# Splitting the 64-column small matmuls of a triangular inversion into halves of 32 loaded columns

## The reference, cut to what matters

```python
l_mat = jnp.where(strict, jnp.einsum('bhncd,bhnjd->bhncj', kb, k) * decay, 0.0)
rhs = jnp.concatenate([v * beta[..., None], kb * jnp.exp(gc)[..., None]], axis=-1)
sol = lax.linalg.triangular_solve(jnp.eye(CHUNK, dtype=F32) + l_mat, rhs,
                                  left_side=True, lower=True, unit_diagonal=True)
```

## Time and profile before

| | |
|---|---|
| median of 3 runs | 2343.88 us (2343.21 to 2346.3) |
| profiled execution, its own time | 2346.62 us |
| its span in the trace | 2345.0 us |
| PE busy | 2319.4 us (99%), 14038 matmul records |
| PEld busy | 1883.7 us (80%) |
| DVE busy | 1270.6 us (54%) |
| ACT busy | 843.1 us (36%) |
| POOL busy | 113.3 us (5%) |
| granted TensorE clock | 0.996 |

### The profile page before, as it was taken

The page is one execution under the profiler, slowest core; times in us unless marked ns, Lnnn a source line. Parts: engine busy times, 40 slices in busy tenths (PEclk is TensorE's granted clock), DMA queues, the critical chain, the costliest instruction groups (busy, mean ns, idle before and its releaser), DMA issues.

```text
span 2345.0 us, 36491 instructions
## 1 busy us (share of the span) xinstructions
PE 2319.4 (99%) x14038; PEld 1883.7 (80%) x14038; DVE 1270.6 (54%) x1777; ACT 843.1 (36%) x1243; POOL 113.3 (5%) x220
## 2 busy tenths in 40 slices
PE   8999999999999999999999999999999999999998
PEld 6888888778777888888878888887777788888886
DVE  4554556675457664433465545667545576443333
ACT  4321234532455443223342223345225555331232
POOL 1000010020000000000000000001000000000000
PEclk9999999999999999999999999999999999999999
DMA  8564563342234344433345645624232352453331
GB/s 321 189 214 152 179 200 120 104 136 96 95 113 149 112 135 152 144 100 101 96 143 183 211 144 188 214 85 125 93 100 90 117 176 93 148 170 99 95 106 58
DMA packets 95152, 325.30 MB, mean 139 GB/s; under 512 B 12904, under 2 KB 13576, under 8 KB 94016
## 3 DMA queue, kind: packets, MB, share of 16 engines
q1 hardware_dynamic: 57456, 216.09, 28.1%
q0 software_dynamic: 23760, 82.48, 11.1%
q10 hardware_dynamic: 13824, 25.17, 3.1%
HBM read 306.34 MB, written 14.73 MB: 137 GB/s over the span
## 4 chain that ended last, share of the span: by engine, by line
PE 95%; DVE 2%; ACT 1%; DMA 1%; issue 0%; SPq 0%; DVEq 0%; POOL 0%; ACTq 0%; POOLq 0%
PE PS L523 84%; PE PS L1058 4%; PE PS L791 2%; DMA ada<-in_ada_first_dram 1%; PE PS L1032 0%; PE PS L783 0%; PE PS L1075 0%; DMA ada_raw<-in_ada_w_dram 0%; PE PS L715 0%; PE PS L742 0%; PE PS L992 0%; PE PS L1041 0%; PE PS L569 0%; PE PS L1008 0%; PE PS L932 0%
## 5 line engine op out<-in xcount | busy, mean ns | idle before, releaser
L1505 DVE TENSOR_TENSOR wl<-raw,wh 128x1024 fp32r<-128x1024 f32 (+2 forms) x360 | 466.0, 1295 | 787.6 <-ACT wh L1136 787.1
L523 PE MATMUL PS<-uh,wh 128*128 128x512 f32 x2176 | 864.4, 397 | 2.2 <-DVE wl L1505 1.9
L523 PE MATMUL PS<-ul,wh 128*128 128x512 f32 x2176 | 848.0, 390 | 0.0
L523 PE MATMUL PS<-uh,wl 128*128 128x512 f32 x2176 | 848.0, 390 | 0.0
L1136 ACT ACTIVATE wh<-raw 128x1024 fp32r<-128x1024 f32 (+2 forms) x360 | 401.5, 1115 | 876.6 <-PE PS L523 862.1
L523 PEld LDWEIGHTS PS<-uh,wh 128*128 128x128 f32 x2176 | 408.4, 188 | 100.9 <-issue 7.3
L523 PEld LDWEIGHTS PS<-uh,wl 128*128 128x128 f32 x2176 | 408.5, 188 | 86.5
L523 PEld LDWEIGHTS PS<-ul,wh 128*128 128x128 f32 x2176 | 408.8, 188 | 82.5 <-issue 1.9
L523 PE MATMUL PS<-hh,wh 128*128 128x512 f32 x736 | 286.9, 390 | 0.0
L523 PE MATMUL PS<-hh,wl 128*128 128x512 f32 x736 | 286.4, 389 | 0.0
L523 PE MATMUL PS<-hl,wh 128*128 128x512 f32 x736 | 286.3, 389 | 0.0
(11 more groups left out here) (277 smaller groups left out, 1627.3 us busy)
## 6 DMA issues: line engine op xcount, KB each, us to landing
raw<-in_ffn_in_dram SPq DMA_DIRECT2D x176, 512.0 KB, 3.5
ada_raw<-in_ada_w_dram POOLq DMA_DIRECT2D x144, 512.0 KB, 3.9
raw<-in_mix_in_dram SPq DMA_DIRECT2D x88, 512.0 KB, 3.6
raw<-in_ffn_out_dram SPq DMA_DIRECT2D x32, 768.0 KB, 4.5
raw<-in_ffn_out_dram SPq DMA_DIRECT2D x32, 640.0 KB, 3.9
g_in<-gates_dram ACTq DMA_DIRECT2D x48, 256.0 KB, 3.1
ada<-in_ada_first_dram SPq DMA_DIRECT2D x8, 1024.0 KB, 16.3
raw<-in_mix_up_dram SPq DMA_DIRECT2D x16, 512.0 KB, 3.6
```

The source lines that it names most:

```text
L523: mm = e.matmul(PS[:, bank, :], w[:, j % 2, k * P:(k + 1) * P], v[:, k, :], start=(k == 0 and w is wh and v is xh), stop=(k == K - 1 and w ...
L1505: TTo(wl[:, j % 2, 0:K * P], raw[:, j, 0:K * P], wh[:, j % 2, 0:K * P], ALU.subtract)\
```

## The change

Each product with 64 loaded columns by 32 streamed is split in two with 32 loaded columns each, by rows of the result (`rows` 0 and 1). The half `rows` loads columns `rows*32` to `rows*32+31` of the same matrix, streams the same 32 columns, and writes 32 partitions instead of 64. A product now names an area of 64 rows by 32 columns of the array: left products use four of eight such areas instead of two of four, updates eight of eight instead of four of four (at the last level four of eight instead of two of four). The number of products doubles, the values do not change.

```diff
-                def half_square(bank, lhs, rhs, lv, which, ts, h, across):
+                def half_square(bank, lhs, rhs, lv, which, ts, h, across, rows):
 
-                    r, o = halves[h], halves[1 - h if across else h]
+                    r, o = halves[h], 64 * (1 - h if across else h) + rows * HALF
                     v = rhs[r, ts, :].rearrange("p (b two w) -> p b two w", two=2, w=2 ** lv)[:, :, which, :]
-                    return e.matmul(PS[o, bank, ts * HALF:(ts + 1) * HALF].rearrange("p (b w) -> p b w", w=2 ** lv),
-                                    lhs[r, ts, :], v, start=True, stop=True)
+                    return e.matmul(PS[o:o + HALF, bank, ts * HALF:(ts + 1) * HALF].rearrange("p (b w) -> p b w", w=2 ** lv),
+                                    lhs[r, ts, rows * HALF:(rows + 1) * HALF], v, start=True, stop=True)
 
                 def left_products(lv):
                     for ts in range(8):
-                        for h in range(2):
-                            mm = half_square(5, cT, Tm, lv, 0, ts, h, True)
+                        for rows in range(2):
+                            for h in range(2):
+                                mm = half_square(5, cT, Tm, lv, 0, ts, h, True, rows)
                     return mm
 
                 def updates(lv):
                     for ts in range(8):
-                        for h in range(2):
-                            mm = half_square(6, Ym[lv], Um, lv, 1, ts, h, False)
-                        if lv < LEVELS - 1:
+                        for rows in range(2):
                             for h in range(2):
-                                mm = half_square(7, Um, Ym[lv], lv, 0, ts, h, True)
+                                mm = half_square(6, Ym[lv], Um, lv, 1, ts, h, False, rows)
+                            if lv < LEVELS - 1:
+                                for h in range(2):
+                                    mm = half_square(7, Um, Ym[lv], lv, 0, ts, h, True, rows)
                     return mm
```

## The result

The changed kernel takes 2350.09 us (median of 20 runs, 2347.48 to 2353.45) against 2343.89 us before (20 runs): ratio 1.0027, 95% interval 1.0021 to 1.0033. It is 6.2 us slower, where 8 us less were forecast. The profiled execution took 2351.63 us, its span is 2350.0 us.

A forecast was written before the change was run, and what follows sets the result against it. PE, busy 99% of the span, was taken to bound the kernel. At 8 ns a record, 24 bursts save 9.5 us and 16 updates lose 1.5, together 8.0 us less: 2336 us predicted from 2343.88, range 2327 to 2351.

The forecast's parts named there:

- how fast PE can take new instructions at all: Unknown price in full updates on eight areas; taken as 8 ns a record, between 3.9 and 14.0 ns.
- 3.544 p - 36.3: Change in us over all 40 bursts at pitch p in ns; turns from gain to loss at 10.2 ns.
- the issue limit: Rival: PE takes small matmuls no faster than now, 12 to 14 ns a record; 13.3 us more, 2357; chance 0.18.
- The waits: Copies between left products and updates stay covered by 1.1 to 1.2 us slack; costed at nothing, about 1 us if failing.
- a cover failed: Sign in the windows over 490 to 600 us: PE waiting for DVE `Tm` or ACT `Ym`.
- The 24 short bursts: 20 left products and 4 last-level updates, 32 records becoming 64, save 0.396 us each, 9.5 us.
- The 16 full updates: Updates of 4 levels, 64 records becoming 128 on eight areas, lose 0.096 us each, 1.5 us.
- The area cycle: Time per record on one area of the array, 58 ns, expected to fall to 31 with 32 loaded columns.
- Shared path: Rival: two 32-column areas within 64 columns take turns; 3.1 us more, 2347; chance 0.19 together with pitches around the turning point.
- areas alone: Rival: eight areas fill as fast as they empty, updates at 3.9 ns; 16.6 us less, 2327.3; chance 0.15.

## Why the prediction was wrong

**The step that failed** is the question which the prediction put as "how fast PE can take new instructions at all". It was priced as a pitch alone, 8 ns a record, with 3.9 and 14.0 ns as its ends, and the sum 3.544 p - 36.3 has no other term in it. As a pitch 8 ns was nearly right: split left products run at 0.563 / 63 = 8.9 ns and updates at 1.098 / 127 = 8.6. But instructions also have a supply, and its price is a time per 256 of them, not per record, and only where they stand close. It is a rival's name with another mechanism: the rival took a limit that slows every burst evenly, would have left left products at 0.9 us, and came to 13.3 us for that. No rate of steady issue gives whole bursts of 0.56 us beside one that stands still for 1.1. That 2350 us lies inside the stated range of 2327 to 2351 is luck: its upper part was there for the half of the issue limit that ends below 12.3 ns, and no burst ran at such a pitch.

How close the trace of before stood to the limit can be worked out. A level from one left product to the next takes about 7 us and holds 64 + 128 instructions of line 791 and some 36 of the large matmuls, about 230, 0.9 of a block, and a block takes 3.45 to 3.73 us: half the time spare. In the changed kernel it holds 128 + 256 + 36, about 420 or 1.6 blocks, 5.9 us of supply in 6.4 us (508.48 to 514.91). On average that still fits; with nine tenths of them in two bursts of together 1.7 us it doesn't, and PE stops where a block's edge falls inside a burst, or in the next one. With full updates whole, 128 + 128 + 36 is 1.1 blocks, 4.1 us. Such sums by level say how near a kernel is to the limit and no more, for the kernel with only the full updates split (1.4 blocks) had 0.8 us of stops and the one with only the left products split (1.1 blocks) 2.8. The chance placing of the edges decides the rest: the same kernel shifted by 128 instructions had its second layer 4.4 us shorter, and its first 2.1 longer.

**The waits**, costed at nothing but for "about 1 us": those named in the prediction, of PE on `Tm` and `Ym`, cost nothing indeed, for PE never waited for either in the inversions. The wait that came was not in the list, because the list held other engines only. The prediction's own test said that a row of PE waiting for DVE or ACT "would show that a cover failed"; the row that came says "issue".

**The 24 short bursts.** 0.396 us each was forecast, 14 of them gave 0.37, and the ten with other small products behind gave 0.24 or 0.22: 7.5 us instead of 9.5. What follows was the part left out. In the trace before, the first products of lines 820 and 765 started among the last records of the left product (the row x26 in the earlier trace rows is cut off by them), and no gap between the last record of line 791 and what came behind was over 0.06 us. Now these products start 0.12 us after the last record of the burst, and those of line 832 too. The prediction counted the bursts as if each stood alone. **The 16 full updates**: 0.096 us each was forecast, 0.155 and 0.275 came, 3.5 us instead of 1.5, since at 127 gaps 0.6 ns more is 0.08 us, and where line 832 follows its gap comes on top. Without the stops the change would have brought 4.0 us, half the forecast; with them it costs 6.2.

**The area cycle** did halve or nearly: from 58 to 8.9 x 4 = 36 ns an area at most, against the forecast 31, load records at 106 ns (forecast 110), matmul records at 193 instead of 219. *Shared path* is out, with 15.6 ns for left products; *areas alone* is out, for updates hold 8.6 ns and not 3.9. Large matmuls kept their pitch and the gaps to them shrank by 0.03 us (0.149 to 0.123). Nothing in the array speaks against the change: bursts on four areas and on eight end up at nearly the same pitch, 8.9 and 8.6 ns, and the added matmuls with 8 streamed columns at 8.5, so it is a floor that no longer depends on the areas. That is why splitting pays for products on two areas and costs for those on four. Which part of PE sets this floor no run here shows.

## What to carry to other kernels

Before splitting matmuls into more and smaller ones, count instructions as a resource of their own: loads and matmuls over a stretch of some 4 us, against 256 of them per 3.5 to 4 us, and the packets of the instruction queue in that stretch of the trace, not over the whole span (in the first inversion 12 packets in 98 us before, 19 in 100 us after). Split the bursts that use few areas, leave those that use four already, and keep dense bursts apart or whole where two of them meet. A wait that ends on "issue" inside a burst, at a fixed count of instructions, was the supply here and not the array, and it can fall on code that was never changed.

## What the runs showed of the hardware

In the kernels with stops the shortest distance between the starts of two packets was 3.3 to 3.8 us; in the kernel before it was 4.3, with a median over its two inversions of 7.7 against 4.4 in the changed one. The kernel with full updates issued twice, which had no stop, came down to 4.2.

A long stop can cost more than itself. In the kernel with the shift in layer 1 alone, behind the stop of 2.38 us the large matmuls ran 0.43 us apart instead of 0.23 for some 3.5 us; the granted clock is 0.59 in the window that holds them, which mixes a stretch at 2.4 GHz with a longer one at 1.2:

```profile
522.46 0.42 PE L523 MATMUL PS<-uh,wl 128*128 128x512 f32 x1
522.69 0.62 PE L523 MATMUL PS<-uh,wh 128*128 128x512 f32 x1
523.10 0.63 PE L523 MATMUL PS<-ul,wh 128*128 128x512 f32 x1
523.53 0.63 PE L523 MATMUL PS<-uh,wl 128*128 128x512 f32 x1
...
522.00:526.00 4.00, 4.00 (x11) 3.20 (x12) 2.64 (x5) 0.00 (x0) 0.77 (x2) 0.59 0.38 130
```

Eight of them lost 1.6 us. The kernel with 128 instructions ahead of both layers showed the same behind its stop of 2.3 us, six matmuls long. Behind the stop of 2.51 us in the key products, where PE had stood idle just as long, the clock stayed full (525.39 to 527.69 us at 0.39 us a matmul), so the length of the stop alone does not tell whether it falls. The Trainium skill, "TensorE: Matmul & The Clock Gate", section "Wait — 56ns, not 53.3ns?", has matmul starts never closer than about 25 ns. The bursts of line 792 held 8.6 to 8.9 ns over 63 and 127 gaps, so the measurement decides against that figure where several areas are in turn.
